# Attention that scales a pair's first head before it takes the last pair's outputs, and head-norm sums right behind the first Fourier features

## What is computed

```python
def token_mix(h, lp, ctx):
    (qa, ka, va, gate_b, gate_c, xb, qc, kc, vc, zc,
     beta_f, beta_b, a_f, a_b, xd) = split_cols(h @ lp['w_in'])
    qa = rms_norm(qa.reshape(Bn, L, N_HEADS_A, HEAD_DIM), lp['q_norm'])
    ka = rms_norm(ka.reshape(Bn, L, KV_HEADS_A, HEAD_DIM), lp['k_norm'])
    ...
    o_a = block_attention(...)                         # softmax(q k / 8) v, 4 query heads, 2 key heads
    o_b = gate_b * depthwise_conv(gate_c * xb, ...)
    o_c, s_end = gated_deltanet(qc, kc, vc, zc, ...)   # conv, SiLU, l2 norm of q and k, recurrence
    o_d = fourier_mix(xd)                              # real part of a 2-D DFT over tokens and channels
    out = jnp.concatenate([o_a, o_b, o_c, o_d], axis=-1) @ lp['w_out']
```

## Time and profile before

| | |
|---|---|
| three runs, us | 3264.95, 3272.24, 3273.00 |
| the profiled execution, its own time | 3271.25 us |
| its span, first to last instruction | 3269.6 us |
| mean granted clock of PE, as a share of full speed | 0.944 |
| busy: PE, PE weight loads, DVE, ACT, POOL | 92%, 87%, 45%, 24%, 8% |

### The profile page before, as it was taken

One profiled execution on the slowest core, in us unless ns is written; L12 is line 12 of the kernel. 1 busy time (PEld: TensorE's weight loads), 2 busy tenths in 40 slices (PEclk: granted clock), 3 DMA queues, 4 the chain that ended last, 5 costly groups with the idle time before them and its releaser, 6 DMA issues.

```text
span 3269.6 us, 58310 instructions
## 1 busy us (share of the span) xinstructions
PE 3021.8 (92%) x24855; PEld 2838.1 (87%) x24855; DVE 1463.9 (45%) x2396; ACT 797.8 (24%) x1155; POOL 249.2 (8%) x297
## 2 busy tenths in 40 slices
PE   5999999898699989999989999989977988999997
PEld 3999999895488889999989999989846878999997
DVE  3433443515466444334454444452255645344444
ACT  2221121322412232221222222222233223212221
POOL 2000000100022100000010000010001211000001
PEclk6999999998789999999999999989977989999998
DMA  7254322221000133454321122212200002221121
GB/s 244 91 180 154 130 89 77 65 65 52 2 4 3 53 116 130 165 170 134 120 78 59 65 69 77 77 65 78 75 4 3 4 2 78 78 70 65 66 68 45
DMA packets 164006, 259.00 MB, mean 79 GB/s; under 512 B 12892, under 2 KB 131908, under 8 KB 163488
## 3 DMA queue, kind: packets, MB, share of 16 engines
q1 hardware_dynamic: 142112, 174.83, 16.4%
q0 software_dynamic: 21760, 82.20, 7.3%
HBM read 253.85 MB, written 3.15 MB: 79 GB/s over the span
## 4 chain that ended last, share of the span: by engine, by line
PE 67%; issue 24%; DVE 3%; ACT 2%; DMA 1%; POOLq 1%; DVEq 1%; POOL 0%; ACTq 0%
PE ps L562 47%; PE ps L549 16%; PE ps L585 2%; POOLq L447 1%; DMA PT<-mod_w 1%; PE ps L806 1%; DMA ub<-mixer_tables 1%; DVE dTF L1688 0%; DVE PT L1339 0%; ACT pTs L1224 0%; DVEq L1340 0%; DVE pexp L1580 0%; DVE cv L1540 0%; DVEq L1616 0%; DVE xT L1757 0%
## 5 line engine op out<-in xcount | busy, mean ns | idle before, releaser
L562 PE MATMUL ps<-hh,uh 128*128 128x320 f32 x3744 | 865.6, 313 | 58.7 <-DVE hl L1366 48.6
L562 PE MATMUL ps<-hl,uh 128*128 128x320 f32 x3744 | 859.4, 311 | 0.0
L562 PE MATMUL ps<-hh,ul 128*128 128x320 f32 x3744 | 858.3, 311 | 0.0
L562 PEld LDWEIGHTS ps<-hh,uh 128*128 128x128 f32 x3744 | 630.6, 190 | 80.1 <-issue 68.7
L562 PEld LDWEIGHTS ps<-hl,uh 128*128 128x128 f32 x3744 | 632.2, 190 | 0.0
L562 PEld LDWEIGHTS ps<-hh,ul 128*128 128x128 f32 x3744 | 631.6, 189 | 0.0
L1331 DVE TENSOR_TENSOR ul<-raw,uh 128x1024 fp32r<-128x1024 f32 x322 | 390.5, 1234 | 341.2 <-ACT uh L1047 325.6
L1376 DVE SCALAR_TENSOR_TENSOR xT<-ps,modT,xT 128x128 f32<-128x128 f32 x736 | 371.5, 547 | 302.4 <-PE ps L562 301.0
L1047 ACT CAST uh<-raw 128x1024 fp32r<-128x1024 f32 x322 | 323.6, 1046 | 550.8 <-PE ps L562 420.6
L1396 DVE SCALAR_TENSOR_TENSOR PT<-ps,PT 128x640 f32<-128x640 f32 x88 | 72.6, 825 | 689.8 <-PE ps L562 689.8
L562 PE MATMUL ps<-gh,uh 128*128 (+1 forms) x1408 | 325.0, 312 | 15.3 <-DVE ul L1331 14.3
(11 more groups left out here) (236 smaller groups left out, 2406.2 us busy)
## 6 DMA issues: line engine op xcount, KB each, us to landing
raw<-ffn_w SPq DMA_DIRECT2D x264, 512.0 KB
PT<-mod_w POOLq DMA_DIRECT2D x72, 1024.0 KB, 9.2
raw<-w_in SPq DMA_DIRECT2D x40, 512.0 KB
raw<-w_out SPq DMA_DIRECT2D x8, 768.0 KB
ub<-mixer_tables POOLq DMA_DIRECT2D x2, 2176.0 KB, 8.6
out<-PT SPq DMA_DIRECT2D x5, 512.0 KB, 2.6
PT<-x_sample SPq DMA_DIRECT2D x4, 512.0 KB, 6.5
raw<-w_out SPq DMA_DIRECT2D x16, 128.0 KB
```

The source lines that it names most:

```text
L562: last = pe.matmul(pair(q)[:, lo:hi], wt[:, wk * P:(wk + 1) * P], mv(mk, lo, hi), start=start and i == 0 and p_ == 0, stop=stop and i == n ...
```

## The change

Nothing is computed anew or left out; the order and one PSUM bank change.

- Attention, DVE: `scales(j)` becomes `scale(j, g)`, and the order `scale(j, 0)`, `heads_out(j - 1)`, `scale(j, 1)`, `peaks(j + 1)`.
- Attention, PE: the value products go to bank 6, and the wait for `pv_used` moves from `turn(j, 0)` to `turn(j, 1)`, which writes from bank 6 on.
- Front, PE: the sums stand right behind `fourier_features(0)`, then `fourier_tokens(0)`, the spread, `fourier_features(1)`, the transposes, the rotations, and `fourier_tokens(1)` behind these. The third rotation (bank 6) first waits until ACT has copied the second features. The wait for the low part of the second token transform moves behind `scores(0)`.
- Front, ACT and DVE: the steps follow in the same order. The reciprocal of the norms stands ahead of the second block of head group B, `fourier_lo(0)` behind it, `fourier_lo(1)` behind the first maxima.

```diff
--- before.py
+++ after.py
@@ -766,12 +766,11 @@
                     pe.transpose(bank(2, 128), lrow[l + 1], ident).then_inc(vecT_done, 1)
                 pe.wait_ge(dft_in.sem, dft_in.at(l, 16))
                 fourier_features(0)
+                head_norm_rows(0, 7)
                 pe.wait_ge(ft_in.sem, ft_in.at(l, 16))
                 fourier_tokens(0)
-                head_norm_rows(0, 7)
+                head_norm_spread(0, 7)
                 fourier_features(1)
-                head_norm_spread(0, 7)
-                fourier_tokens(1)
 
 
                 pe.wait_ge(bc_used.sem, bc_used.at(l, 7))
@@ -782,8 +781,10 @@
                 pe.transpose(bank(1, 128, 128), PT[:, C_KA, 0:P], ident)
                 pe.transpose(bank(1, 128, 256), ckr, ident).then_inc(tr_done.sem, 1)
                 for n, c in enumerate((C_QA, C_QA + 1, C_KA)):
+                    if n == 2:
+                        pe.wait_ge(f1_used.sem, f1_used.at(l, 2))
                     fp32(bank((2, 3, 6)[n]), tcol(T_ROT), PT[:, c, CTX:T]).then_inc(rot_done.sem, 1)
-                pe.wait_ge(f_lo.sem, f_lo.at(l, 2))
+                fourier_tokens(1)
                 pe.wait_ge(roped.sem, roped.at(l, 1))
                 pe.wait_ge(tr_used.sem, tr_used.at(l, 1))
 
@@ -800,7 +801,7 @@
 
                 def turn(j, g):
                     pe.wait_ge(p_ready.sem, p_ready.at(l, 2 * j + g + 1))
-                    if j and g == 0:
+                    if j and g == 1:
                         pe.wait_ge(pv_used.sem, pv_used.at(l, j))
                     for t in range(5 if j >= 2 else 1):
                         mm = pe.transpose(tiles5(4 + 2 * g)[:, t, :], pexp[j % 2][:, g, t * P:(t + 1) * P], ident)
@@ -811,9 +812,10 @@
                     pe.wait_ge(pT_used.sem, pT_used.at(l, 2 * j + 2))
                     for t in keys:
                         for g in range(2):
-                            mm = fp32(bank(4, P)[half(g), :], vtok[:, t if j >= 2 else 5, half(g)], pTs[g][:, t, :], t == 0, t == keys[-1])
+                            mm = fp32(bank(6, P)[half(g), :], vtok[:, t if j >= 2 else 5, half(g)], pTs[g][:, t, :], t == 0, t == keys[-1])
                     mm.then_inc(pv_done.sem, 1)
                 scores(0)
+                pe.wait_ge(f_lo.sem, f_lo.at(l, 2))
                 for j in range(10):
                     turn(j, 0)
                     if j < 9:
@@ -1189,16 +1191,15 @@
                         fourier_features(0)
                     if n == 3:
                         sq.then_inc(sq7_ready.sem, 1)
-                        fourier_tokens(0)
                 act.activation(PT[:, C_ZC:C_ZC + 2, :], PT[:, C_ZC:C_ZC + 2, :], ACT.Silu)
                 act.drain()
                 act.wait_ge(nr_done.sem, nr_done.at(l, 1))
                 act.activation(rrow[0:14, 1, :], pair(0)[0:14, :], ACT.Sqrt, bias=tb[0:14, T_SC + 1:T_SC + 2],
                                scale=tb[0:14, T_SC:T_SC + 1]).then_inc(nq_ready.sem, 1)
-                fourier_features(1)
+                fourier_tokens(0)
                 act.wait_ge(ob_ready.sem, ob_ready.at(l, 1))
                 act.copy(hh[:, 2:4, :], PT[:, C_GB:C_GB + 2, :]).then_inc(ob_hi.sem, 1)
-                fourier_tokens(1)
+                fourier_features(1)
 
 
                 act.wait_ge(tr_done.sem, tr_done.at(l, 1))
@@ -1527,17 +1529,17 @@
 
                 for c in range(2):
                     if c:
-                        fourier_lo(0)
+                        ve.wait_ge(nq_ready.sem, nq_ready.at(l, 1))
+                        ve.reciprocal(rrow[0:14, 0, :], rrow[0:14, 1, :]).then_inc(nrow_ready.sem, 1)
                     ve.tensor_tensor(PT[:, C_XB + c, :], PT[:, C_XB + c, :], PT[:, C_GC + c, :], ALU.mult)
                     ve.drain()
                     conv(PT[:, C_GC + c, :], PT[:, C_XB + c, :], lambda j, c=c: V_CONVB + 2 * j + c)
                     ve.drain()
                     i = ve.tensor_tensor(PT[:, C_GB + c, :], PT[:, C_GB + c, :], PT[:, C_GC + c, :], ALU.mult)
                 i.then_inc(ob_ready.sem, 1)
-
-
-                ve.wait_ge(nq_ready.sem, nq_ready.at(l, 1))
-                ve.reciprocal(rrow[0:14, 0, :], rrow[0:14, 1, :]).then_inc(nrow_ready.sem, 1)
+                fourier_lo(0)
+
+
                 for n, c in enumerate(NORMS):
                     ve.wait_ge(bc_done.sem, bc_done.at(l, n + 1))
                     if n < 3:
@@ -1548,7 +1550,6 @@
                     i.then_inc(bc_used.sem, 1)
                 ve.wait_ge(ob_hi.sem, ob_hi.at(l, 1))
                 ve.tensor_tensor(hl[:, 2:4, :], PT[:, C_GB:C_GB + 2, :], hh[:, 2:4, :].bitcast(F32), ALU.subtract)
-                fourier_lo(1)
 
 
                 ve.wait_ge(mt_in.sem, mt_in.at(l, 80))
@@ -1570,28 +1571,31 @@
                         ve.drain()
                         ve.tensor_scalar(ast[:, a4 + 1:a4 + 2], ast[:, a4:a4 + 1], -HEAD ** -0.5, None, ALU.mult).then_inc(nmax_ready.sem, 1)
 
-                def scales(j):
+                def scale(j, g):
                     w = T if j >= 2 else P
-                    for g in range(2):
-                        a4 = 4 * (2 * (j % 2) + g)
-                        ve.wait_ge(p_exp.sem, p_exp.at(l, 2 * j + g + 1))
-                        ve.reciprocal(ast[:, a4 + 3:a4 + 4], ast[:, a4 + 2:a4 + 3])
-                        ve.drain()
-                        ve.tensor_scalar(pexp[j % 2][:, g, 0:w], pexp[j % 2][:, g, 0:w], ast[:, a4 + 3:a4 + 4], None, ALU.mult).then_inc(p_ready.sem, 1)
+                    a4 = 4 * (2 * (j % 2) + g)
+                    ve.wait_ge(p_exp.sem, p_exp.at(l, 2 * j + g + 1))
+                    ve.reciprocal(ast[:, a4 + 3:a4 + 4], ast[:, a4 + 2:a4 + 3])
+                    ve.drain()
+                    ve.tensor_scalar(pexp[j % 2][:, g, 0:w], pexp[j % 2][:, g, 0:w], ast[:, a4 + 3:a4 + 4], None, ALU.mult).then_inc(p_ready.sem, 1)
 
                 def heads_out(j):
                     n, c = j // 2, j % 2
                     ve.wait_ge(pv_done.sem, pv_done.at(l, j + 1))
                     hs = hh[:, c, n * P:(n + 1) * P]
-                    ve.tensor_copy(hs, bank(4, P))
+                    ve.tensor_copy(hs, bank(6, P))
                     ve.drain()
-                    ve.tensor_tensor(hl[:, c, n * P:(n + 1) * P], bank(4, P), hs.bitcast(F32), ALU.subtract).then_inc(pv_used.sem, 1)
+                    ve.tensor_tensor(hl[:, c, n * P:(n + 1) * P], bank(6, P), hs.bitcast(F32), ALU.subtract).then_inc(pv_used.sem, 1)
                 peaks(0)
+                fourier_lo(1)
                 for j in range(10):
-                    scales(j)
+                    scale(j, 0)
+                    if j:
+                        heads_out(j - 1)
+                    scale(j, 1)
                     if j < 9:
                         peaks(j + 1)
-                    heads_out(j)
+                heads_out(9)
 
 
                 ve.tensor_scalar(PS[32:40, :], PS[32:40, :], adt[32:40, 1:2], None, ALU.add).then_inc(sp_x.sem, 1)
```

## The result

The changed kernel takes 3235.24 us (median of 4 runs, 3229.06 to 3246.76), against 3271.61 us for the kernel before in the same session. The ratio is 0.9898, with a 95% interval of 0.9874 to 0.9921: about 1% faster, 36 us. Run once more in a later session, it took 3233.47 us, ratio 0.9887 (0.9873 to 0.9901). The profiled execution was the slowest of its four, 3246.76 us, with a span of 3245.1 us.

A forecast was written before the change was run, and what follows sets the result against it. PE was taken to bound the kernel in the changed stretches, front and attention (256.1 us). Cycle 17.6, fronts 3.3 and clock in attention 3.6 sum to 24.5 us off 3271.25, so 3246.8 us; range 3233 to 3261 us.

The forecast's parts named there:

- The likeliest case: Whole kernel: the forecast of 3246.8 us, 0.75% faster, chance 0.76.
- the clock in attention: Attention: PE's clock higher from a warm entry and fewer falls, 1.8 us per layer, 3.6 us; bounds 0 and 8.
- The cycle: Attention, wide pairs: earlier scaling saves 1.16 us per step; with narrow and last pairs 8.8 us per layer, 17.6 in all.
- The two steps out of the narrow pairs: Attention: each gains between 0 and 1.16 us, taken as 0.7 us, together 1.4 us per layer.
- The warm entry: Attention's start: PE comes from 7 us of full work, so first scores and turns are fast, about 1.0 us per layer.
- The falls: Attention, later cycles: PE's denser work spares part of the later clock falls, taken as 0.8 us per layer.
- The fronts: Front of each layer: 57.8 us; with the first turn's loss, 3.3 us gained in all; bounds 8 gained, 12 lost.
- step 3: Front: the sums, now started from idleness, take 9.7 us instead of 7.71; token-transform rate put at 7.3 us.
- step 5: Front: first norm multiplication at 2385.9, spread ends about 2396.9 instead of 2397.13, with 0.7 us back from a later clock fall.
- the sums stay cold: Rival, front: the sums do nothing for the clock and take 15.4 us; costs 11.4 us, 3258 us; chance 0.12.
- the cycle finds another bound: Rival, attention: the second head's slack is used up, half the cycle gain lost, 8.8 us, 3256 us; chance 0.08.
- the clock stays down and the kernel gets slower: Rival, attention: five more cycles per layer run cold at 8.8 us instead of 5.14, giving 3287 us; chance 0.04.

The follow-up runs named there:

- padded: Changed kernel with two idle DVE operations ahead of the first head's reciprocal in each wide pair but the first: 3261.46 us, ratio 0.9972.
- early_table: Changed kernel with a one-column exponential on ACT ahead of the last high part, so its table loads earlier: 3243.81 us, measured once.
- wide_spread: Changed kernel with the spread's matmuls reading 128 rows of weights instead of 14, the added rows zero: 3228.63 us, ratio 0.9862.
- bank4: Changed kernel with value products back in bank 4 and the pv_used wait back before the first head's transposes: 3252.64 us, ratio 0.9951.
- best: Changed kernel with first token transform split around the sums, late group B block, 128-row spread, early table load, rotations before transposes: 3215.25 us, ratio 0.9829.
- front_only: Changed kernel with attention as in the kernel before, so only the front is new: 3265.94 us, ratio 0.9987.

## Why the prediction was right, and which term was off

The likeliest case came true, by its own mechanism. The time is 11.6 us under the forecast and inside the range, but near its lower end of 3233 us (the second measurement, 3233.47 us, lies 0.5 us above it). The miss is one term, the clock in attention.

- **The cycle.** Forecast 1.16 us off every wide cycle; measured 6.30 to 5.14 us, to the hundredth, with 0.30 us of idle time left where 0.31 was forecast. The two steps out of the narrow pairs were put at 1.4 us per layer; they gave 1.9, of which 0.5 is the warm entry. The last pair waits for its second head as forecast: from its first turn to the end of attention it takes 4.88 us, against 4.31 us before with its pieces warm (5.40 in layer 1, less 1.09 for value products at the low clock), a loss of 0.57 where 0.7 was forecast. Together 8.1 + 1.4 - 0.6 = 8.9 us per layer, 8.8 forecast.
- **The clock in attention: the mis-sized term.** It had two parts. The warm entry, put at 1.0 us per layer, gave 0.6 and 1.1, as read from one profile each. The falls, put at 0.8 us per layer as "a part of the later falls", were the error: all of them behind the first wide cycle went. Attention is shorter by 14.82 us in layer 0 and 13.05 in layer 1. Take off the 8.9 us, add the 0.8 that the first turn lost, take off the warm entry, and 6.1 and 3.8 us are left, 9.9 us where 1.6 was forecast. The steps show them: in layer 1 those of 7.93 and 7.84 us against 6.30, and the cold value products of the last pair. `padded` has 6.6 us of them back with the longer cycle. The whole term was 3.6 us with bounds of 0 and 8; measured it is 9.9 + 1.7 = 11.6 us, outside them. With 9.9 in place of 1.6 the forecast sum of 24.5 us becomes 32.8, against 33.6 in the stages.
- **The fronts.** Forecast 57.8 us in both layers; measured 57.39 and 57.15. The steps hold one by one: idle time ahead of the sums 6.3 us (6.30), the sums 9.7 (9.59), first norm multiplication 30.5 us into the front (2374.47 - 2344.39 = 30.1), the spread's end 41.5 (41.8), the wait for cached data 0.5 (0.65), the rope hidden. Two small slips are in step 3 and step 5. By its own rate eight long and two short matmuls come to 7.8 us and not 7.3; measured are 7.58 and 7.48. And the 0.7 us that a later fall of the clock should give back in the spread did not come: its last twenty records ran at 0.51 (10.80 us, 2.16 per chunk). The table load and the high part ahead of it cost the first turn 0.7 us by forecast, 0.81 measured. Of this 0.48 goes with the load alone, as `early_table` shows; then the low part on DVE, which the forecast had fit beside it, is what the turn waits for. Fronts less that loss: 4.1 us gained, 3.3 forecast.
- **The rest.** In the profiled execution the sum of 24.5 us and the 24.5 us less of span agree by accident: the stages gave 33.6, and the stages behind them, the recurrences above all, took 9 back. The comparison that counts is of the medians, and there the forecast was too small.
- **The rivals.** That the sums stay cold: they took 9.59 and 9.52 us and not 15.4, and the granted clock rose under them from 0.50 to 1.00. That the cycle finds another bound: PE waits 0.30 us, for `pexp` alone. That the clock stays down and the kernel gets slower: it is 0.90 over attention.

The Trainium skill, "TensorE: Matmul & The Clock Gate", section "What's actually happening", has a throttled default state that activity releases. For the denser cycle this has the right sign, and the trace agrees (0.77 and 0.81 became 0.90 and 0.91). For the spread it doesn't: PE was busy through 10.80 us at 0.51, and it took `wide_spread` to get 1.00.

## What to carry to other kernels

Where a profile shows an engine's clock falling now and then in a steady cycle, price a shorter cycle twice: once for the wait that goes, and once for the falls that may go with it. Here the second was 9.9 us and the first 17.8. `padded`, with cycles 1.33 us longer, gives 6.6 us of it back, and `bank4`, with cycles 0.63 us longer, loses 3.2 us per layer to low clock in its first wide cycles. A value product's bank and a scaling's place in a queue are worth a look wherever the cycle's last wait ends with an operation whose input has been ready for some time.

Before costing a move of work in a front, list which of the pieces run below the full clock while busy. From the changed kernel to `best` the front of layer 1 lost 12.0 us: 5.4 in waits (6.30, 1.19 and 0.65 against 2.75) and 6.6 in pieces that run faster.

## What the runs showed of the hardware

- Matmuls with 14 rows of weights ran at a granted clock of 0.51 through 10.80 us without a pause; with the same products widened to 128 rows, the added weights being zeros, the clock was 1.00 and the same twenty records took 5.92 us. The sums, with 128 rows of weights and 14 columns, are not of this kind: they began cold and ended warm, 9.59 us.
- Within attention there were no falls after the second wide pair in cycles of 5.14 us and of 5.77 us, and falls in cycles of 6.30 and 6.47 us. The state at the entry changed the short cycle's start by 0.6 to 1.1 us and nothing later, which is less than the first wide cycle scatters by itself (5.14 to 7.43 us in kernels with the same attention); in `front_only` the old cycle became slower after a warm entry, for a reason left open.
- A stage that no edit touched, the recurrence, took between 198.9 and 207.6 us in the profiles of these kernels, and 206.8 and 201.6 us for one and the same kernel. A single profiled span can hide 9 us this way, while the four stage windows of that kernel came to 222.5 and 222.4 us in the same two executions.
